# Layer 1 of a two-layer hybrid diffusion backbone: its dense weights stream through two ring slots instead of three, and the third slot takes a half-matrix of an expert at the opening of the layer

## What is computed

```python
for l in range(2):
    mod = silu(c) @ w_ada[l] + b_ada[l]              # w_ada: 1024 x 6144; six vectors sh1, sc1, gt1, sh2, sc2, gt2
    h = rms_norm(x) * (1 + sc1) + sh1
    z = h @ w_in[l]                                  # conv, two attentions, three gate blocks
    outs = (gated_conv(z), neighbourhood_attention(z), window_attention(z))
    merged = sum(sigmoid(gate[i]) * (outs[i] @ w_branch[l][i]) for i in range(3))
    x = x + gt1 * (merged @ w_out[l])
    h = rms_norm(x) * (1 + sc2) + sh2
    # 16 experts, each takes 32 of 256 tokens:
    ye = (silu(xe @ w_gate[e]) * (xe @ w_up[e])) @ w_down[e]
    x = x + gt2 * scatter(ye * gate)
return rms_norm(x)
```

## Time and profile before

| what | before |
|---|---|
| median of 3 runs | 1841.15 us (1837.36, 1841.15, 1841.23) |
| the profiled execution | 1836.87 us |
| its span (first to last instruction) | 1834.7 us |
| PE busy | 1683.3 us, 92% of the span |
| HBM read | 539.13 MB, 295 GB/s over the span |
| granted TensorE clock, mean | 0.98 |

### The profile page before, as it was taken

How to read it: one execution, slowest core, us unless ns; L and a number is a source line. 1 busy time by engine, 2 the same in 40 slices (tenths; PEclk the granted TensorE clock), 3 DMA queues, 4 the chain that set the end, 5 groups by cost and what they waited for, 6 DMA issues and landing times.

```text
span 1834.7 us, 26514 instructions
## 1 busy us (share of the span) xinstructions
PE 1683.3 (92%) x10854; PEld 978.0 (53%) x10854; DVE 768.2 (42%) x1746; ACT 478.0 (26%) x1052; POOL 113.1 (6%) x149
## 2 busy tenths in 40 slices
PE   6999999999998999999998799999999997776876
PEld 3887777776664333333232498877883332222322
DVE  4455566675434233333323665577753222111111
ACT  4224455552133100000000534455441000000001
POOL 1012210000001000000000012300001000000000
PEclk9999999999999999999999899999999998999999
DMA  9353231127779999999999774237899999999996
GB/s 352 110 140 93 86 92 58 35 81 259 266 278 364 409 428 428 428 428 428 427 427 427 271 204 143 75 128 261 284 365 387 427 426 426 427 425 425 426 426 285
DMA packets 152035, 543.83 MB, mean 296 GB/s; under 512 B 10026, under 2 KB 92400, under 8 KB 126700
## 3 DMA queue, kind: packets, MB, share of 16 engines
q1 hardware_dynamic: 149104, 535.35, 74.4%
q0 software_dynamic: 2400, 6.16, 1.3%
q10 hardware_dynamic: 412, 0.64, 0.1%
HBM read 539.13 MB, written 2.98 MB: 295 GB/s over the span
## 4 chain that ended last, share of the span: by engine, by line
PE 69%; DMA 23%; DVE 3%; ACT 2%; issue 1%; SPq 1%; POOL 0%; DVEq 0%; ACTq 0%
PE bank L2158 20%; PE bank L2019 12%; PE bank L2020 11%; PE bank L2021 11%; DMA ring<-in_w_exp_down 8%; DMA ring<-in_w_exp_gate 7%; DMA ring<-in_w_exp_up 5%; DMA spare<-in_w_exp_gate 3%; PE bank L2132 2%; PE bank L2048 2%; PE bank L2071 2%; PE bank L1934 2%; PE bank L2058 2%; PE bank L2187 1%; DMA ring<-in_w_in 1%
## 5 line engine op out<-in xcount | busy, mean ns | idle before, releaser
L2158 PE MATMUL bank<-ring,XEP 128*32 128x256 f32 (+1 forms) x2384 | 385.2, 618 | 37.9 <-DMA ring<-in_w_exp_gate 21.4
L2019 PE MATMUL bank<-HH,WH 128*128 128x512 f32 (+1 forms) x864 | 311.5, 361 | 3.4 <-DVE HL L1627 2.5
L2020 PE MATMUL bank<-HL,WH 128*128 128x512 f32 (+1 forms) x864 | 300.1, 347 | 0.0
L2021 PE MATMUL bank<-HH,WL 128*128 128x512 f32 (+1 forms) x864 | 299.6, 347 | 0.0
L2158 PEld LDWEIGHTS bank<-ring,XEP 128*32 128x32 f32 (+1 forms) x2384 | 114.9, 131 | 277.9 <-issue 229.6
L1598 DVE TENSOR_TENSOR WL<-ring,WH 128x1024 fp32r<-128x1024 f32 (+1 forms) x172 | 185.7, 1082 | 133.1 <-ACT WH L1362 132.4
L1856 DVE TENSOR_TENSOR X<-X,bank 128x512 f32<-128x512 f32 x184 | 114.0, 683 | 190.3 <-PE bank L2187 100.1
L2019 PEld LDWEIGHTS bank<-HH,WH 128*128 128x128 f32 x864 | 163.5, 189 | 50.9 <-issue 24.4
L1362 ACT CAST WH<-ring 128x1024 fp32r<-128x1024 f32 (+1 forms) x172 | 158.1, 927 | 101.4 <-PE bank L2021 64.7
L2158 PE MATMUL bank<-ring,HIDT 128*32 128x256 f32 (+1 forms) x1232 | 152.6, 477 | 31.9 <-DMA ring<-in_w_exp_down 31.9
L2021 PEld LDWEIGHTS bank<-HH,WL 128*128 128x128 f32 x864 | 163.7, 189 | 21.0
(11 more groups left out here) (244 smaller groups left out, 1950.9 us busy)
## 6 DMA issues: line engine op xcount, KB each, us to landing
ring<-in_w_exp_gate SPq DMA_DIRECT2D x55, 2048.0 KB, 31.0
ring<-in_w_exp_up SPq DMA_DIRECT2D x49, 2048.0 KB, 34.5
ring<-in_w_exp_down SPq DMA_DIRECT2D x48, 2048.0 KB, 36.2
ring<-in_w_ada SPq DMA_DIRECT2D x48, 1024.0 KB, 7.7
ring<-in_w_in SPq DMA_DIRECT2D x40, 1024.0 KB, 6.5
split_slot<-in_w_exp_up SPq DMA_DIRECT2D x8, 2048.0 KB, 29.1
split_slot<-in_w_exp_down SPq DMA_DIRECT2D x8, 2048.0 KB, 33.6
ring<-in_w_in SPq DMA_DIRECT2D x28, 512.0 KB, 5.5
```

Of the source, the lines that this page charges most:

```text
L2019: mm(t, wh, hi[:, k, 0:b.n], start=k == 0, stop=False)
L2020: mm(t, wh, lo[:, k, 0:b.n], start=False, stop=False)
L2021: last = mm(t, wl, hi[:, k, 0:b.n], start=False, stop=k == b.kk - 1)
L2158: last = mm(out_bank[tw * g:tw * g + tw, 0:nw], stationary(k), w[:, g::G] if spread else w[:, nw * g:nw * g + nw], start=k == 0, stop=k == ...
```

## The change

In layer 1 `STREAM` goes from 3 to 2 and slot 2 moves from the last place of the expert order to the first. Slot 2 is filled with expert chunk 0 by a new `expert_load` behind the last load of the convolution weights; the slots 9, 4, 10, 3, 6, 7, 0, 5, 8 and 1 each take the chunk after the one that they had. Layer 0 is as it was.

```diff
-STREAM = [2, 3]
-ORDER = [[2, 3, 6, 7, 4, 5, 8, 0, 1], [9, 4, 10, 3, 6, 7, 0, 5, 8, 1, 2]]
+STREAM = [2, 2]
+ORDER = [[2, 3, 6, 7, 4, 5, 8, 0, 1], [2, 9, 4, 10, 3, 6, 7, 0, 5, 8, 1]]
...
         if last:
+            expert_load(*[o for a, b, o in P.occupants if a <= SLOT * 2 < b])
             expert_load(Step(o_ready=("ht_ready", 2 * KD)))
```

## The result

| | before | changed |
|---|---|---|
| median | 1840.21 us (4 runs) | 1861.95 us (4 runs, 1858.85 to 1862.71) |
| ratio | 1 | 1.0122, 95% interval 1.0109 to 1.0136 |
| profiled span | 1834.7 us | 1860.4 us |

That is 22 us slower, where 14 were forecast. The two profiled executions differ already before the change can act: layer 0 is the same program, and SP issues the first load of layer 1 at 1005.87 us in the one and at 1009.91 us in the other. Over the nine traces of this document its moment ranges from 1004.9 to 1009.9 us, so a difference of whole times carries up to 5 us that arise before layer 1. The last expert byte lands 815.8 us after it before (1821.66), and 837.1 us after it now (1847.03): 21.3 us, the whole result.

The account below looks back on a forecast made before the run. Layer 1's experts were taken to end when their last byte lands: 14.7 us of later chunks, less 5.7 us coming back, plus 5 us of PE delay, is 14 us; on the mean of 1839.2 us, 1853 us, range 1842 to 1863.

Parts of the forecast that it names:

- Part 3: At output block 0: the first half of `w_out` waits for gate d = 7, so PE waits 4.9 us.
- Part 4: Before the experts: the next chunk waits for the tile of `w_ada` 10; transfers stand still for some 15 us.
- the rival with more waits: Waits beyond those found, at layer 1's opening or in the window attention: another 8 us or more, 1861 us and above; chance 0.12.
- Part 1: Opening of layer 1: one chunk moves from 1382.87 to about 1055, alone worth 4.9 us, its issue there costed at nothing.
- the rival of 1834 us: Faster: the early chunk's 4.9 us is won and nothing is lost, 1834 us; chance 0.06.
- Part 2, the window attention: At `w_ada` 6 and `sq3`: late second half (PE waits 2.3 us) and ACT's in-order queue, together 5 us of PE delay.
- Part 2, the groups costed at nothing: Other modulation groups: second halves are issued 8 us or more ahead of their matmuls, so no cost.
- The part that comes back: Between the eleventh and seventeenth chunks: the queued chunks close a hole the transfers had before, giving back 5.7 us.
- No change: Rival: a hole of only a few us, or a later stretch that catches up, 1836 to 1843 us; chance 0.10.
- only the hole: Rival: both PE waits hidden, 4 us, 1843 us (1848 with one wait); chance 0.20 for these.

Follow-up runs that it names:

- Experiment 7: The kernel before, three slots, with the first chunk of slot 2 left out of the loads but for one 32 KB piece: 1838.88 us, ratio 1.0006.
- experiment 1: The kernel before with layer 1's stream cut to two slots, slot 2 still last in the order: 1864.01 us, ratio 1.0139.

## Why the prediction was right or wrong

The direction, the mechanisms of parts 3 and 4 and the order of SP's queue were right. The size was 14 us and came out as 21 to 22, outside the 1849 to 1859 that the forecast gave itself and at the time of the rival with more waits (1861 and above). That it still lies within 1842 to 1863 is owed to the width left for that rival, not to the sum.

The forecast has PE 9.9 us late at the experts (5 in the window attention, 4.9 at `w_out`) and about 4 us of queue on top. Measured are 16.6 and 4.7 us. The 16.6 divide into 9.5 us up to the end of the window attention, 1.1 us in branch 3, 4.8 us at output block 0 and 1.2 us behind it. Step by step:

**Part 1, the early chunk.** Costed at nothing at the opening of the layer: right as far as one trace can tell. ACT waited 2.9 and 3.6 us for weights of the values and the query there, and PE's shift up to 1256 is 0.3 us, no more than executions differ by. But its worth was misjudged. I called it 4.9 us alone, and the rival of 1834 us rested on it. Experiment 7 puts it at nothing within the interval. In the changed kernel it does count, as one chunk fewer in the late queue (experiment 1), but this only makes a hole smaller that the change itself opens.

**Part 2, the window attention. This is the term that was mis-sized.** I took 5 us. At the matmuls on `w_ada` 6, PE waited 7.2 us and not 2.3. I had seen that ACT would stand until `sq3`'s weights land, and which evictions and copies stand behind it, but let PE start `w_ada` 6 on its own data. What failed is the step "PE waits 2.3 us": the tile of `w_ada` 6 needs a PSUM bank, and the eviction that frees it was one of those behind ACT's cast. The weights of `sq3` also landed later than I put them: at 1267.61, which is 1263.6 in before's time, and not 1262. And the wait costs clock, a term that the sum does not have. The sixteen matmuls took 3.64 us, against 1.92, and the windows of the changed kernel give the granted clock as

```profile
1260.00:1266.00 6.00, 1.80 (x16) 1.60 (x14) 0.00 (x0) 0.00 (x0) 0.00 (x0) 1.00 0.80 257
1266.00:1273.00 7.00, 3.99 (x18) 1.02 (x19) 2.95 (x6) 2.37 (x3) 0.00 (x0) 0.52 0.74 232
1273.00:1280.00 7.00, 7.00 (x56) 5.49 (x55) 5.45 (x18) 4.28 (x15) 0.00 (x0) 0.99 0.84 299
```

so the engine stood for 7.2 us and the matmuls behind that ran at the lower of its two levels, 1.2 instead of 2.4 GHz, which puts the mean from 1266 to 1273 at 0.52. Wait and clock are 7.2 + 1.7 = 8.9 us. The Trainium skill (Perfetto Trace Analysis, section Matmul Optimizations) says that the matmul engine scales its power by its utilization, so that matmuls should come back to back in batches; this row agrees, in that the granted clock is low right behind the idle time.

**Part 2, the groups costed at nothing.** For the modulation groups themselves that held. But gate d = 2 of branch 3 waited: its cast found its weights 2.5 us late, and a later one 3.2 us late, with 0.8 us of it on PE at L2020 and 1.1 us of shift.

**Part 3, `w_out`.** Expected 4.9 us of wait, measured 4.6, and nearly 6 us of shift with what follows. The clock is in this too: the matmuls behind the wait take 0.41 us each, where those of the same block had 0.28, and by the end of the output blocks PE has lost another 1.0 us. Issue to landing of the first half was 7.8 us (1348.50 to 1356.25), near the 8.0 of the earlier trace rows. The prediction's other figure, an estimate of 6.8 us by the Trainium skill (DMA: Bandwidth & Descriptors, section Anatomy of one DMA), is too short here, and that section gives its fit for transfers that GpSimd issues, where SP issued this one. The measurement decides.

**Part 4, the hole.** Expected: last `w_ada` to the first data of slot 0 some 15 us. Measured: `w_ada` lands at 1389.1, the first chunk at 1408.9, less its own 4.9 us: 14.9 us. The part that comes back, expected 5.7 us, is the difference between 27.0 us at the eleventh chunk and 21.3 at the last byte. Together with PE's delay this was the right account, only the reading behind it was too narrow: I asked when the transfers run without a hole. The question that gives all nine kernels is when PE begins, and how many chunks are queued then.

**The rivals.** "Faster" has no ground left, for the reason in part 1. "No change" and "only the hole" fell with PE's two long waits, which are in the rows shown. "More waits than I found" is in part what happened: not more places, but the same one deeper.

## What to carry to other kernels

In this kernel a prefetch was worth nothing, since all buffers were full when their reader began (experiment 7): before moving a transfer ahead, look whether the queue already stands still there (360 and 401 GB/s around 1400 where 427 was the rate). And a slot taken from a stream is paid at the loads that are largest against what is left, here 2048 KB of `w_ada` or `w_out` in a stream of 4096 KB: list for each the last reader of the bytes that it lands on. Where a late load is read by an in-order engine, ask what that engine frees further down its queue, PSUM banks above all.

## What the runs showed of the hardware that was not expected

The wait of 7.2 us put TensorE to half its clock for the matmuls that followed (0.52 from 1266 to 1273), which made a wait of 7.2 us cost 8.9. The wait of 4.6 us at output block 0 did the same: 0.41 us for a matmul that took 0.28 before, and a granted clock of 0.72 from 1356 to 1362:

```profile
1356.00:1362.00 6.00, 3.32 (x16) 3.35 (x17) 4.55 (x7) 3.21 (x4) 0.00 (x0) 0.72 1.13 381
```

In the dense stage the trace of before shows a granted clock of 1.00 from 1240 to 1300.
